# A mixture-of-experts pass on one core: one branch per unit for further blocks, their activations transposed a pass later, and six experts per loop turn in place of two

## The chip, the cores and the metric

One core of one Trainium2 chip runs the whole program. The metric is the device time of one execution in microseconds (us), the median of several runs.

## What is computed

A decoder layer for 512 tokens of width 1024: a token-mixing sub-layer (two attention branches), then a channel-mixing one, a mixture of 32 experts of which each token uses four. The change touches only the experts:

```python
logits = (ht @ w_router + b_router); top_val, top_idx = lax.top_k(logits, TOP_K)   # TOP_K = 4, 32 experts
# token slots are sorted by expert, each expert's group padded to blocks of 128 rows
def expert_block(args):
    xb, e = args
    gu = xb @ w_gate_up[e] + b_gate_up[e]            # 1024 -> 2 x 1024
    return clamped_swiglu(gu) @ w_down[e] + b_down[e]
ys = lax.map(expert_block, (xs, block_e)).reshape(n_rows, d) * row_w
out = zeros.at[row_tok].add(ys)
```

Each expert has about 64 tokens, so most have one block of 128 rows ("the first block"). Where a block beyond it is filled it is called a further block; up to three are provided for. In the profiled data three experts, numbers 7, 19 and 28, have one further block each: the trace shows 35 gathers for 32 experts.

## The kernel before

**Units and halves.** An expert has 12 MB of float32 weights in 12 *halves* of 1 MB (128 x 2048): eight for gate and up (`N_GU = 8`), four for down (`N_D = 4`). Two halves make one *unit*, 512 output columns accumulated in a PSUM bank. Each float32 factor is split in two parts of lower precision, so that a product is three matmuls (`multiply`, lines 1051 to 1053: `wh` x `xh`, `wl` x `xh`, `wh` x `xl`); a half is 12 matmuls of 128x512, a unit 24, with one bias matmul ahead (`biased`, line 1057).

**Engines.** SyncE loads the halves into eight slots `rawm` (`load`; a slot is free when `half_used` says that TensorE has used the half eight before). ScalarE rounds each to `wh` (four slots, line 1154, free when the half four before is used), VectorE forms `wl` = `rawm` - `wh` (line 1225). GpSimd gathers the tokens of an expert into `xy`, and scatters its outputs to `expert_rows` (lines 1315 and 1334); a gather waits for the scatter that frees the buffer.

**A pass.** `body(e, ...)` on TensorE is: the four gate/up units of expert e; the transposes of the tokens of e + 1 (`tokens_transposed`); the two down units of e - 1; the transposes of the activations of e (`act_transposed`). ScalarE and VectorE copy each transposed block into a high part (`xh`, `ah`) and a low part (`xl`, `al`). ScalarE's order in a body is written out: 12 weight splits, with the gate at halves 1 and 5, the tokens' high part at 7, the outputs of e - 1 at 9 and 11, and the activations' high part (`act_high`) last; VectorE's likewise.

**Further blocks.** Counts are data. Each engine loads the number of further blocks of an expert from `nk` into a register (`Expert`, line 874), and code for them stands inside branches: `further` (line 909) skips three copies of the work if there is none. In `blocks` the further ones come ahead of the first block, in `first_then_further` behind it. On TensorE, `gate_up_half_used` and `down_half_used` call it once for each of the 12 halves; with the two kinds of transposes a body has 14 such branches.

**The loop.** `passes` runs body 0, then the bodies of experts 1 to 30 two per turn in a hardware loop (line 943, 15 turns, with a hint for the backward branch), then body 31. Every engine but GpSimd runs through it, each on its own; GpSimd has a loop of its own, which doesn't change.

## Time and profile before

| | |
|---|---|
| median of 3 runs | 1965.25 us (1964.48 to 1971.41) |
| profiled execution | 1966.11 us, span of its instructions 1964.3 us |
| TensorE (PE) busy | 1700.9 us, 87% |
| VectorE (DVE), ScalarE (ACT), GpSimd (POOL) busy | 67%, 52%, 12% |
| granted TensorE clock, mean | 0.925 |
| DMA | 498.81 MB, 254 GB/s |

The profile comes from one execution. Matmuls overlap, so a matmul's duration (0.39 us) is longer than the distance between two (0.23 us). "Issue" is time in which an engine waited for nothing that the profile shows, neither a semaphore nor a buffer; its sequencer (marked q) may still be at work on branches and registers. The granted clock is given as a share: 1.00 is 2.4 GHz, 0.50 is 1.2 GHz. Until about 480 us attention runs, then the experts, and from 1903 us on the outputs are combined.

### The profile page before, as it was taken

What the parts mean: (1) busy time and instruction counts of PE and PEld (TensorE: products, weight loads), DVE (VectorE), ACT (ScalarE), POOL (GpSimd) and SP (SyncE); (2) the same over time, 40 slices, a digit from 0 to 9 for tenths busy, and PEclk for the clock granted to TensorE, in tenths of its full rate; (3) what the DMA queues carried; (4) which work ended last, traced back from release to release, by engine and by line L of the source; (5) the groups of instructions that cost most, each with busy time, mean ns of one, the idle gap of its engine ahead of it and who ended that gap; (6) DMA issues with size and microseconds to landing.
All of it is one profiled execution on the core that took longest, in us unless ns stands there. A gap on an engine that the chain in (4) does not pass through costs nothing.

```text
span 1964.3 us, 24736 instructions
## 1 busy us (share of the span) xinstructions
PE 1700.9 (87%) x7526; PEld 1315.3 (67%) x7527; DVE 1317.5 (67%) x1024; ACT 1029.6 (52%) x922; POOL 229.2 (12%) x232
## 2 busy tenths in 40 slices
PE   6999976685488999999999999999999998989860
PEld 1788854443376877787777877878787787778650
DVE  0444468644478778586877877866687787566645
ACT  2322234511366766465766766745576676455530
POOL 2000000102201001011111101101100111001110
PEclk9999987797699999999999999999999999999885
DMA  7675440012689999687989988977798899667735
GB/s 230 218 246 185 150 120 1 28 65 76 230 300 333 326 327 337 221 300 279 353 309 323 353 315 319 370 255 259 273 373 317 315 362 331 219 237 274 274 135 220
DMA packets 245582, 498.81 MB, mean 254 GB/s; under 512 B 16795, under 2 KB 17927, under 8 KB 244737
## 3 DMA queue, kind: packets, MB, share of 16 engines
q1 hardware_dynamic: 228288, 458.26, 65.5%
q0 software_dynamic: 14448, 34.73, 5.2%
q8 instruction: 217, 3.56, 0.7%
q10 hardware_dynamic: 2610, 2.11, 0.3%
q14 instruction: 19, 0.16, 0.0%
HBM read 490.23 MB, written 27.09 MB: 263 GB/s over the span
## 4 chain that ended last, share of the span: by engine, by line
PE 69%; issue 5%; DVE 3%; DMA 2%; ACT 1%; POOL 1%; POOLq 0%; ACTq 0%; DVEq 0%
PE ps L1051 20%; PE ps L1052 20%; PE ps L1053 19%; PE ps L621 3%; PE ps L993 3%; PE ps L1057 3%; DMA x1e<-x_after_mixing 1%; ACT wh L1154 1%; DVE wl L1225 1%; DMA xy<-h_ffn,icur 1%; DMA expert_rows<-xy,icur 1%; PE ps L641 0%; DVE yo L1388 0%; PE ps L634 0%; ACT h2t L692 0%
## 5 line engine op out<-in xcount | busy, mean ns | idle before, releaser
L1225 DVE TENSOR_TENSOR wl<-rawm,wh 128x2048 fp32r<-128x2048 f32 x384 | 876.2, 2290 | 318.9 <-ACT wh L1154 316.9
L1154 ACT ACTIVATE wh<-rawm 128x2048 fp32r<-128x2048 f32 x384 | 736.2, 1918 | 488.9 <-PE ps L1053 488.8
L1051 PE MATMUL ps<-wh,xh 128*128 128x512 f32 x1120 | 477.8, 427 | 0.0
L1052 PE MATMUL ps<-wl,xh 128*128 128x512 f32 x1120 | 447.4, 399 | 0.0
L1053 PE MATMUL ps<-wh,xl 128*128 128x512 f32 x1120 | 446.3, 399 | 0.0
L1053 PEld LDWEIGHTS ps<-wh,xl 128*128 128x128 f32 x1120 | 216.9, 194 | 48.2
L1052 PEld LDWEIGHTS ps<-wl,xh 128*128 128x128 f32 x1120 | 217.9, 195 | 45.6
L1051 PEld LDWEIGHTS ps<-wh,xh 128*128 128x128 f32 x1120 | 219.3, 196 | 41.6
L1051 PE MATMUL ps<-wh,ah 128*128 128x512 f32 x560 | 235.0, 420 | 0.0
L1052 PE MATMUL ps<-wl,ah 128*128 128x512 f32 x560 | 220.4, 394 | 0.0
L1053 PE MATMUL ps<-wh,al 128*128 128x512 f32 x560 | 220.1, 393 | 0.0
L1331 POOL COPY icur<-stab 128x1 int32 (+1 forms) x35 | 49.6, 1417 | 1026.4 <-ACT xy L1194 1026.3
L1057 PE MATMUL ps<-bparts,sel 96*128 96x512 bf16 x210 | 85.1, 405 | 70.3 <-issue 54.8
L1053 PEld LDWEIGHTS ps<-wh,al 128*128 128x128 f32 x560 | 106.4, 190 | 23.3
L1052 PEld LDWEIGHTS ps<-wl,ah 128*128 128x128 f32 x560 | 106.8, 191 | 21.9
L1051 PEld LDWEIGHTS ps<-wh,ah 128*128 128x128 f32 x560 | 107.5, 192 | 20.3
L1711 DVE TENSOR_TENSOR wlf<-raw,whf 128x2048 fp32r<-128x2048 f32 (+1 forms) x18 | 39.1, 2174 | 100.7 <-ACT whf L1487 100.7
L1057 PEld LDWEIGHTS ps<-bparts,sel 96*128 (+1 forms) x210 | 20.5, 98 | 115.3 <-issue 110.3
L1590 PE MATMUL ps<-whf,hh 128*128 128x512 f32 (+1 forms) x192 | 71.3, 372 | 0.0
L1592 PE MATMUL ps<-whf,hl 128*128 128x512 f32 (+1 forms) x192 | 71.1, 370 | 0.0
L1591 PE MATMUL ps<-wlf,hh 128*128 128x512 f32 (+1 forms) x192 | 71.0, 370 | 0.0
L993 PE MATMUL ps<-ident,xy 128*128 128x128 f32 x280 | 38.4, 282 | 33.2 <-DMA xy<-h_ffn,icur 26.8
(224 smaller groups left out, 1658.2 us busy)
## 6 DMA issues: line engine op xcount, KB each, us to landing
rawm<-in_w_gate_up SPq DMA_DIRECT2D x256, 1024.0 KB, 6.6
rawm<-in_w_down SPq DMA_DIRECT2D x128, 1024.0 KB, 6.3
raw<-in_w_ada SPq DMA_DIRECT2D x24, 1024.0 KB, 5.3
raw<-in_w_in SPq DMA_DIRECT2D x16, 1024.0 KB, 5.2
yt<-expert_rows POOLq DMA_DIRECT2D x4, 2048.0 KB, 9.1
wo<-in_w_out SPq DMA_DIRECT2D x2, 2048.0 KB, 17.0
bias_vectors_repeated<-bias_vectors POOLq DMA_DIRECT2D x1, 2304.0 KB, 15.8
xs<-in_x ACTq DMA_DIRECT2D x1, 2048.0 KB, 24.5
```

Of the source, the lines that this page charges most:

```text
L621: ins = nc.tensor.matmul(ps[:, 2 * b + half, :], src[:, k, t * P:(t + 1) * P], wo[:, 4 * b + k, half * UN:(half + 1) * UN], start=(k == 0) ...
L993: ins = nc.tensor.transpose(turned(b)[:, k // 4, (k % 4) * P:(k % 4 + 1) * P], src[:, k * P:(k + 1) * P], ident[:])
L1051: nc.tensor.matmul(dst, a_h[:, b, kk, :], wh[:, place.split(v), k, :], start=False, stop=False)
L1052: nc.tensor.matmul(dst, a_h[:, b, kk, :], wl[:, place.slot(v), k, :], start=False, stop=False)
L1053: ins = nc.tensor.matmul(dst, a_l[:, b, kk, :], wh[:, place.split(v), k, :], start=False, stop=kk == KC - 1)
L1057: nc.tensor.matmul(dst, sel[:, bass.ds(e, 1)].to_broadcast([96, P]), bias, start=True, stop=False)
L1154: nc.scalar.activation(flat(wh[:, place.split(v), :, :]), flat(rawm[:, place.slot(v), :, :]), ACT.Copy).then_inc(wh_done, 1)
L1225: nc.vector.tensor_tensor(flat(wl[:, place.slot(v), :, :]), flat(rawm[:, place.slot(v), :, :]), flat(wh[:, place.split(v), :, :]), ALU.sub ...
L1331: nc.gpsimd.tensor_copy(icur[:, 1, b:b + 1], stab[:, b, bass.ds(x.e + 1, 1)]).then_inc(scur[m], 1)
L1590: nc.tensor.matmul(dst, a_h, b_h, start=first, stop=False)
L1591: nc.tensor.matmul(dst, a_h, b_l, start=False, stop=False)
L1592: return nc.tensor.matmul(dst, a_l, b_h, start=False, stop=last)
```

## The change

Three edits. The loop of `passes` holds six bodies per turn (`TURN = 6`, five turns for experts 1 to 30). On TensorE `gate_up_used` and `down_used` work on a whole unit: one branch for the further blocks, which do both halves, then the first block's two halves. The activations of the first block are transposed ahead of the last 12 matmuls of the second down unit; those of further blocks in the next pass, behind its first gate/up unit (`further_act_transposed`), with their copies after half 1 on ScalarE and VectorE, and TensorE's wait for them ahead of the fourth unit (`further_acts_split`). The bank pair `turned(0)` serves all activations.

```diff
+TURN = 6
     def passes(eng, body):
 
         body(0, Place(0, 0), False)
-        with nc.Fori(0, E // 2 - 1, engines=[eng.engine], hint_back_edge=True) as k:
-            body(2 * k + 1, Place(3 * k + 1, 0), True)
-            body(2 * k + 2, Place(3 * k + 2, 4), True)
-        k = E // 2 - 1
-        body(E - 1, Place(3 * k + 1, 0), True)
+        with nc.Fori(0, (E - 2) // TURN, engines=[eng.engine], hint_back_edge=True) as k:
+            for i in range(TURN):
+                body(TURN * k + 1 + i, Place(3 * TURN // 2 * k + (3 * i + 2) // 2, 4 * (i % 2)), True)
+        body(E - 1, Place(3 * (E // 2 - 1) + 1, 0), True)
...
                     if b == 1 and not begins:
-                        acts = Expert(pe, e - 1).prefix() + START
...
-                        pe.wait_ge(al_done[1], acts)
...
-        def act_transposed(x, last):
+        def first_act_transposed(x, last):
 
             pe.wait_ge(xl_done[0], x.e + (1 if last else 2) + START)
+            pe.wait_ge(act_ready[0], x.count(T_GU, 1, 0))
+            transposed(turned(0), actv[:, 0, :], at_done[0])
+
+        def further_act_transposed(x):
             def work(b):
...
+                pe.wait_ge(act_ready[1], x.count(T_GU, 1, b))
+                pe.wait_ge(al_done[0], x.count(1, 0, 0))
+                pe.wait_ge(al_done[1], x.count(1, 0, b) - 1)
+                transposed(turned(0), actv[:, b, :], at_done[1])
+            x.further(work)
+
+        def further_acts_split(x):
+            with pe.If(x.more >= 1):
+                x.prefix()
+                pe.wait_ge(al_done[1], x.all_more(1, 0))
+                pe.sem_inc(passed, 1)
...
+        def gate_up_used(x, has_d, place, v):
...
+                biased(dst, x.e, bias)
+                for h in range(2):
+                    pe.wait_ge(wl_done, place.count(v + h))
+                    ins = multiply(dst, place, v + h, b, h, xh, xl)
+                ins.then_inc(gu_more, 1)
+            x.further(further)
+
+            if v == 0:
+                pe.wait_ge(xl_done[0], x.count(1, 0, 0))
+            if t == 0 and has_d:
+                pe.wait_ge(y_half_copied[up], x.e - 1 + START)
+            elif t:
+                pe.wait_ge((u_ready if up else g_ready)[0], x.count(T_GU, 0, 0))
+            biased(summed(0, up), x.e, bias)
+            for h in range(2):
+                pe.wait_ge(wl_done, place.count(v + h))
+                multiply(summed(0, up), place, v + h, 0, h, xh, xl).then_inc(half_used, 1)
...
+            for h in range(2):
+                if t and h and after is not None:
+                    first_act_transposed(after, is_last(after.e))
+                pe.wait_ge(wl_done, place.count(v + h))
+                multiply(summed(0, t), place, v + h, 0, h, ah, al).then_inc(half_used, 1)
...
         def body(e, place, has_d):
             x = Expert(pe, e)
             last = is_last(e)
...
+            before = None
+            for v in range(0, N_GU, 2):
+                if v == 2 and has_d:
+                    before = Expert(pe, e - 1)
+                    further_act_transposed(before)
+                if v == 6:
+                    if has_d:
+                        further_acts_split(before)
                     nxt = None if last else Expert(pe, e + 1)
...
+                gate_up_used(x, has_d, place, v)
             if not last:
                 tokens_transposed(nxt, e + 1)
...
-            act_transposed(x, last)
+            if has_d:
+                for t in range(U_D):
+                    down_used(before, x, place, N_GU + 2 * t, t)
+            else:
+                first_act_transposed(x, last)
...
                 split_high(place, v + SPL)
+                if v == 1 and has_d:
+                    act_high(before, before.further)
```

## Rows read from the trace of the kernel before

**Rows 1.** The page, part 4: the chain that ended last, by engine.
```profile
PE 69%; issue 5%; DVE 3%; DMA 2%; ACT 1%; POOL 1%; POOLq 0%; ACTq 0%; DVEq 0%
```

**Rows 2.** Windows by stage, experts 1 to 31: busy (x count) per engine, clock, DMA.
```profile
core 0: us, PE busy (x) PEld busy (x) DVE busy (x) ACT busy (x) POOL busy (x), PEclk, DMA share, GB/s
...
556.30:1903.00 1346.70, 1270.44 (x5685) 1020.85 (x5686) 1008.84 (x576) 842.17 (x577) 158.70 (x132) 0.97 0.84 301
```

**Rows 3.** Waits of TensorE, 560 to 1900: total us, times, longest.
```profile
PE ps L1057 <- issue: 54.6, 20, 7.2
...
PE ps L1057 <- DVE wl L1225: 5.2, 2, 4.4
```

**Rows 4.** The chain before expert 15: start us, us, what.
```profile
1136.46 4.47 issue
1140.93 0.60 PE ps L1057
```

**Rows 5.** Line 909, 1133 to 1142: duration ns min/median/max, first and last start.
```profile
L909 PEldq COMPARE_BRANCH  x3: 231/233/4590, 1133.2 to 1141.1; - x3
L909 ACTq COMPARE_BRANCH  x2: 92/95/98, 1135.6 to 1136.5; - x2
```

**Rows 6.** Line 943, the same stretch, TensorE's sequencer.
```profile
L943 PEldq COMPARE_BRANCH  x1: 1316/1316/1316, 1133.6 to 1133.6; - x1
```

**Rows 7.** DMA queues, 1062 to 1141: packets, MB, share of 16 engines.
```profile
q8 instruction: 13, 0.21, 1.0%
```

**Rows 8.** Windows of TensorE: body 14; first unit of expert 15; first unit of 14.
```profile
core 0: us, PE busy (x), PEclk, DMA share, GB/s
1099.51:1135.42 35.91, 35.91 (x167) 1.00 0.99 354
...
1140.93:1148.94 8.01, 8.01 (x25) 0.69 0.27 90
1100.38:1106.06 5.68, 5.68 (x27) 1.00 0.90 310
```

**Rows 9.** Windows, transposes' start to second unit: expert 14; 8; 19's first unit alone.
```profile
1099.51:1106.06 6.55, 6.55 (x34) 1.00 0.92 321
...
854.38:862.60 8.22, 7.58 (x42) 1.00 0.76 243
1299.50:1310.89 11.39, 11.39 (x50) 1.00 0.61 221
```

**Rows 10.** The same at ten backward branches: before 9, 29, and sum of ten.
```profile
903.37:911.27 7.90, 6.71 (x34) 1.00 0.51 165
...
1744.12:1759.87 15.75, 9.97 (x42) 0.78 0.52 178
sum 126.45, PE 86.78; mean PE 8.68
```

**Rows 11.** The same before 7, 13, 19, 25, 31: 13, and sum of five.
```profile
1057.13:1070.14 13.01, 9.25 (x34) 0.74 0.56 198
...
sum 66.61, PE 51.69; mean PE 10.34
```

**Rows 12.** Line 874, 775 to 779.5: TensorE's loads of a count.
```profile
L874 PEldq TENSOR_LOAD <-nk x2: 298/300/302, 775.9 to 777.4; - x2
```

**Rows 13.** Timeline of TensorE: transposes of expert 7's further tokens.
```profile
779.32 1.09 PE L993 MATMUL ps<-ident,xy 128*128 128x128 f32 x8 [3.23 <-issue]
```

**Rows 14.** Line 909 in body 14, 1100 to 1135.
```profile
L909 PEldq COMPARE_BRANCH  x13: 222/227/2173, 1100.0 to 1133.2; - x13
```

**Rows 15.** Timeline of GpSimd in body 14: the gather.
```profile
1111.78 2.63 POOL L1315 DMA_INDIRECT xy<-h_ffn,icur  x1 [0.90 <-POOL icur L1312]
```

**Rows 16.** DMA issues, 1110 to 1123: median us from issue to landing.
```profile
xy<-h_ffn,icur POOLq DMA_INDIRECT x1, 8.4
```

**Rows 17.** Timelines of TensorE: token transposes in bodies 30 and 9.
```profile
1829.67 1.97 PE L993 MATMUL ps<-ident,xy 128*128 128x128 f32 x8 [5.23 <-DMA xy<-h_ffn,icur]
...
928.79 1.09 PE L993 MATMUL ps<-ident,xy 128*128 128x128 f32 x8 [0.26 <-DMA xy<-h_ffn,icur]
```

**Rows 18.** Window of TensorE: experts 21 and 22.
```profile
1408.76:1484.51 75.75, 72.11 (x333) 1.00 0.99 362
```

**Rows 19.** Timeline of TensorE: the entry into the loop, expert 1.
```profile
556.31 0.61 PE L1057 MATMUL ps<-bparts,sel 96*128 96x512 bf16 x1 [0.26 <-issue]
```

More of the change, by code:

```diff
@@ L989, in experts_pe, with transposed @@
         pe.wait_ge(nk_ready, 1)
-        def transposed(b, src, done):
+        def transposed(banks, src, done):
             for k in range(KC):
-                ins = nc.tensor.transpose(turned(b)[:, k // 4, (k % 4) * P:(k % 4 + 1) * P], src[:, k * P:(k + 1) * P], ident[:])
-            ins.then_inc(done[min(b, 1)], 1)
+                ins = nc.tensor.transpose(banks[:, k // 4, (k % 4) * P:(k % 4 + 1) * P], src[:, k * P:(k + 1) * P], ident[:])
+            ins.then_inc(done, 1)
         def tokens_transposed(x, e):
@@ L1057, in biased, with further @@
             nc.tensor.matmul(dst, sel[:, bass.ds(e, 1)].to_broadcast([96, P]), bias, start=True, stop=False)
-        def gate_up_half_used(x, has_d, place, v):
-            t, up, h = v // 4, v // 2 % 2, v % 2
-            pe.wait_ge(wl_done, place.count(v))
-            def work(b):
+        def gate_up_used(x, has_d, place, v):
+            t, up = v // 4, v // 2 % 2
+            bias = bparts[:, up * D + UN * t:up * D + UN * (t + 1)]
+            def further(b):
                 dst = summed(b, up)
-                if v == 0 and b == 0:
-                    pe.wait_ge(xl_done[0], x.count(1, 0, 0))
-                if v == 0 and b:
+                if v == 0:
                     outputs = Expert(pe, x.e - 1).prefix() * U_D + START if has_d else None
@@ L1087, in work @@
-                ins = multiply(dst, place, v, b, h, xh, xl)
-                if b == 0:
-                    ins.then_inc(half_used, 1)
-                elif h:
-                    ins.then_inc(gu_more, 1)
-            x.blocks(work)
-        def down_half_used(x, after, place, v, d):
-            t, h = d // 2, d % 2
-            pe.wait_ge(wl_done, place.count(v))
-            def work(b):
+                if b == 1 and t:
+                    pe.wait_ge((u_ready if up else g_ready)[1], x.count(T_GU, 0, b))
+                elif b > 1 and up:
+                    pe.wait_ge(g_ready[1], x.count(T_GU, t, b))
+                elif b > 1 and t:
+                    pe.wait_ge(u_ready[1], x.count(T_GU, 0, b))
@@ L1100, in work, with down_used, further @@
+            biased(summed(0, up), x.e, bias)
+            for h in range(2):
+                pe.wait_ge(wl_done, place.count(v + h))
+                multiply(summed(0, up), place, v + h, 0, h, xh, xl).then_inc(half_used, 1)
+        def down_used(x, after, place, v, t):
+            bias = bparts[:, 2 * D + UN * t:2 * D + UN * (t + 1)]
+            def further(b):
                 dst = summed(b, t)
-                if d == 0 and b == 0:
-                    pe.wait_ge(al_done[0], x.count(1, 0, 0))
@@ L1103, in work @@
-                if d == 0 and b:
+                if t == 0:
                     gate_ups = x.before + x.more if after is None else x.before + x.more + after.more
@@ L1110, in work @@
                     pe.wait_ge(u_ready[1], gate_ups * T_GU + START)
[L1111 to L1122 removed]
+                elif b > 1:
+                    pe.wait_ge(y_copied[1], x.count(U_D, 0, b))
+                biased(dst, x.e, bias)
+                for h in range(2):
+                    pe.wait_ge(wl_done, place.count(v + h))
+                    ins = multiply(dst, place, v + h, b, h, ah, al)
+                ins.then_inc(d_more, 1)
+            x.further(further)
+            if t == 0:
+                pe.wait_ge(al_done[0], x.count(1, 0, 0))
+            pe.wait_ge((u_ready if t else g_ready)[0], (x.e + (1 if after is None else 2)) * T_GU + START)
+            biased(summed(0, t), x.e, bias)
+            for h in range(2):
+                if t and h and after is not None:
+                    first_act_transposed(after, is_last(after.e))
+                pe.wait_ge(wl_done, place.count(v + h))
+                multiply(summed(0, t), place, v + h, 0, h, ah, al).then_inc(half_used, 1)
         tokens_transposed(Expert(pe, 0), 0)
@@ L1173, in gate, with act_high @@
             x.blocks(work)
[L1175 removed]
+        def act_high(x, blocks):
             def work(b):
@@ L1196, in outputs, with at_once @@
             x.blocks(work)
+        def at_once(work):
+            work(0)
         tokens_high(Expert(act, 0))
@@ L1214, in body @@
                     outputs(before, v // 2 - 4, place, v, after)
-            act_high(x)
+            act_high(x, at_once)
         passes(act, body)
         end = Expert(act, E - 1)
+        act_high(end, end.further)
         outputs(end, 0, LAST, 1, None)
@@ L1267, in experts_dve, with at_once @@
         dve.wait_ge(nk_ready, 1)
+        def at_once(work):
+            work(0)
         tokens_low(Expert(dve, 0))
@@ L1280, in body @@
                 split_low(place, v + SPL)
+                if v == 1 and has_d:
+                    act_low(before, before.further)
             if not has_d:
                 tokens_low(Expert(dve, e + 1))
-            act_low(x)
+            act_low(x, at_once)
         passes(dve, body)
+        end = Expert(dve, E - 1)
+        act_low(end, end.further)
     def experts_pool(pool):
```

66 lines of the change are left out of this document (10 added, 56 removed).

## The prediction

> **What bounds the kernel now.** I start with the page's chain of work that ended last. TensorE holds 69% of it and "issue" 5%: time in which TensorE waited for nothing that the profile shows [rows 1]. The windows by stage put two thirds of the run, 1346.70 us, into the passes of experts 1 to 31, with TensorE busy for 1270.44 us of them at a mean clock of 0.97 [rows 2]. So TensorE bounds this stage, and the only thing to win is its 76 us of idle time and the slow clock behind it. TensorE's waits there are few: 54.6 us in 20 waits before the bias matmul (line 1057) are "issue"; the weights (`wl`) make it wait twice, 5.2 us [rows 3].
>
> Where are the "issue" waits? The chain around one of them, before expert 15, shows 4.47 us of issue from 1136.46 on and then the first bias matmul of the new expert [rows 4]. In the same 9 us the branch instructions tell why: TensorE's sequencer needs 1.3 us for the loop's backward branch (line 943), then 4.59 us for one skip branch of line 909, the first after it, where the median one takes 0.23 us [rows 5, 6]. The loop target was there in time; the code that the first skip leads to was not. The instruction queue moved 13 packets and 0.21 MB, so 16 KB each, in the two passes of that turn [rows 7]: TensorE's code doesn't stay on the chip, it streams. ScalarE takes 0.1 us for the same branches [rows 5].
>
> The price of one turn is more than the gap: the first unit behind it takes 8.01 us at clock 0.69, where an undisturbed one takes 5.68 at 1.00 (0.5 is 1.2 GHz, 1.00 is 2.4) [rows 8]. So I measure from the transposes' start to the second unit's start: 6.55 us undisturbed, 8.22 with 16 transposes, 11.39 plus 0.87 where the new expert has a further block [rows 9].
>
> Inside a turn nothing is lost: body 14 runs 35.91 us with TensorE busy for 35.91 [rows 8]. That is 144 matmuls, six biases and 16 transposes at full rate.
>
> **Part 1, six experts per turn.** Thirty experts (1 to 30) make 15 turns now: 14 backward branches and one exit. Afterwards there are 5 turns: 4 backward branches (before experts 7, 13, 19, 25) and the exit before 31. The ten that go (before 3, 5, 9, 11, 15, 17, 21, 23, 27, 29) last 126.45 us in sum [rows 10]; undisturbed they would last 9 x 6.55 + 8.22 = 67.2. Gain: **59.2 us**. The five that stay hold 66.61 us against 3 x 6.55 + 2 x 12.26 = 44.2, so 22.4 us of loss remain [rows 11]; those before 7 and 19 cost only 2 us each, because these experts have a further block and the first skip isn't taken.
>
> **Part 2, first activations transposed ahead of the last 12 matmuls of the down product.** The work (0.87 us) is the same. Its input waits were over long before (none shows within body 14 [rows 8]), and ScalarE reads the result after the last output as now, so nothing later comes earlier. They wait for the next expert's `xl` and for this one's activations, and the last 12 matmuls and the next unit queue behind them; both are done some 8 us before. What changes is the cover of a backward branch. The sequencer runs ahead of TensorE: the branch behind the last transposes starts at 1133.2, TensorE ends them at 1136.46 [rows 4, 5], a lead of some 3 us. Eight transposes last 0.87 us, 12 matmuls 2.7, so the queue holds more time later. I take 1.4 us off each of the three long edges left (13, 25, 31): **-4 us**, between 0 and -8. At the end, after expert 31, the wait for `al` stays: it hangs on ScalarE's last weight split and output, not on the transposes. Nothing.
>
> **Part 3, further activations in the next pass.** Three experts (7, 19, 28) have one further block. Today its 8 transposes follow the first block's directly: 8.22 - 6.55 = 1.67 us, of which 0.87 is the work. Behind the first unit the sequencer is ahead and the other 0.8 us are covered: **-2 us** in all, bounds 0 and -2.4. The added wait for `al` stands ahead of the fourth unit, with all of that unit queued behind it, 11 us after the transposes; two copies on ScalarE and VectorE fit in, so it costs nothing. Without that cover it would be 2 to 3 us in each of three passes. The token transposes of a further block lose one prefix sum, two register loads of 0.3 us each and their arithmetic, out of gaps of issue of up to 3.23 us [rows 12, 13]: another **-2 us** over three experts.
>
> **Part 4, one branch per unit.** A body has 12 + 2 taken skips now, 6 + 3 later. At 0.23 us each this would be 5 x 31 x 0.23 = 36 us, if it were exposed. It isn't: body 14 holds 13 such branches, one of them 2.17 us long, and TensorE isn't idle for any [rows 8, 14]. I book zero; the cover is the lead of the sequencer over the matmuls. The Trainium skill ("Advanced Engine Details and Errata", Control Flow Timing) gives 108 ns for a compare-and-branch; by it the same count would be 17 us, and equally hidden. The trace disagrees with the figure for taken skips, with 0.23.
>
> The other side is that skips become longer. I estimate from the source: a body holds some 1330 tensor instructions (12 halves x 4 copies x 24, plus transposes and biases) and perhaps 200 for control; two bodies over 13 to 14 fetches [rows 7] give some 225 per 16 KB. A skip then jumps about 95 instructions (0.4 of a fetched block) now and 170 (0.75) later, while a unit runs 56. Run and skip together remain one block per 5.7 us, against a full miss of 4.59. So fetches keep up on average, but a landing near a block's end exposes what the lead doesn't cover, at most 4.59 - 3 = 1.6 us. Six bodies have six alignments against two now. I book **+4 us**; bounds: 0 (body 14's loss; less isn't possible) and 1 us in every body, +31.
>
> The Trainium skill's rule here ("Runtime: NRT & Kernel Launch", Instruction fetch mechanics) is that a taken branch whose target lies outside the two resident pages must fetch it first. The trace agrees at the loop (4.59 us). Taken alone, it speaks for fewer turns and against longer skips; that is the slower rival below.
>
> **Part 5, what comes late next.** Tokens. Body 14's gather is issued at 1111.78 and takes 8.4 us, so it lands at 1120.2 [rows 15, 16], and its transposes are due after four units of 5.7 us from 1100.38 on, at 1123.2: 3 us of slack, 0.9 less once the other transposes move. Two bodies behind an expert with a further block the two scatters delay it: body 30 waits 5.23 us, and body 9, which had a backward branch to hide it, 0.26 [rows 17]. Body 9 loses that cover, 7.90 - 6.55 = 1.35 us [rows 10], and the 0.87 of the moved transposes: with the 0.26 that is 2.5 us. Body 21 in the same way +0.9, body 30 +0.9 more, small ones +1: **+5 us**, up to +15.
>
> ScalarE, VectorE and SyncE get three times the code per turn and may have to fetch at the five edges, which no row of theirs shows now (0.1 us [rows 5]). By TensorE's row a miss is 4.59 us. The order on all queues is unchanged, and the weights are prepared far enough ahead that TensorE waits for them twice in the stage [rows 3]. **+2 us**, bounds 0 and 5 x 4.6 = 23, nearer the lower, since TensorE mostly stands still at the same edges.
>
> Sum: -59.2 - 4 - 2 - 2 + 0 + 4 + 5 + 2 = **-56.2 us**. The profiled execution took 1966.1 us (span 1964.3), 0.9 above the median of 1965.25, so 1965.25 - 56.2 = **1909 us**.
>
> **Rivals.** *A, DMA takes over as the bound.* Each 6 us stall is also a rest for DMA: share 0.5 to 0.58 in those windows [rows 10, 11], 0.99 in body 14 [rows 8]. If a body needed 37 us of transfers against 35.9, the 25 or so undisturbed bodies would cost 1.1 us each: 27 us, result 1936. Against it: experts 21 and 22 ran 75.75 us with no long stall, DMA at 0.99 and 362 GB/s, TensorE busy for 72.11 [rows 18], and body 14 needs only 354 GB/s. Chance 0.11.
>
> *B, slower: longer skips expose the fetch inside bodies.* Place: the skip branch of each of 6 x 31 units. It cancels the gain from 0.3 us exposed per unit on. If every second unit exposed a full miss less the lead, 4.59 - 3.3 = 1.3 us, it would be 93 x 1.3 = 121 us on top of the forecast: 2030. For it: skips of 0.75 block nearly always cross into the next one. Against: 2.17 us waits are hidden now, and the fetch rate needed falls slightly. Chance 0.05; half of it (0.3 exposed) would be no change.
>
> *C, partial exposure:* 1 us per body, +27 over the forecast: 1936. Chance 0.10.
>
> *D, the change doesn't do what it says:* the stall belongs to the amount of code, not to the backward branch, and reappears inside the long turn: 1958 or so. Against: in all turns it sits on the first skip behind line 943, and the entry into expert 1 shows only 0.26 us [rows 19]. Chance 0.03.
>
> *E, better:* the loop target lies early in its block, so the first longer skip still lands in it: the edges 13, 25 cost nothing, 1899. Chance 0.08.
>
> Forecast 0.63. **Range:** 1890 to 1942 takes in E and the upper ends of A and C, leaves out B and D. A measurement here tells about 0.5% (10 us) from no change. Faster 0.92, same 0.03, slower 0.05.
>
> **What the new profile would show.** Right: "issue" before line 1057's successor falls from 20 waits to about 7, with 3 over 3 us; clock over the stage 0.99; the stage near 1290 us; DMA share there 0.88. Wrong: TensorE idle in front of biases inside turns with PE branches over 4 us (B, C); waits for `wl` or ScalarE waiting for rawm landings (A); tokens late by over 3 us in many bodies.

## The result, and the profile after

| | median us | range, runs |
|---|---|---|
| before, beside it | 1968.26 | 1964.48 to 1971.41, 4 |
| after | 1945.6 | 1941.11 to 1948.16, 4 |

Ratio 0.9883, 95% interval 0.9852 to 0.9914. The kernel became faster, by 22.7 us or 1.2%, where 56 were forecast, and 1945.6 lies outside the range of 1890 to 1942. The profiled execution took 1943.69 us, span 1941.2.

The page of the changed kernel, its parts 3 and 4: the queue that brings code to TensorE (packets, MB, share), and the chain by engine, to be held against [rows 1].

```profile
q8 instruction: 201, 3.29, 0.7%
...
PE 65%; DMA 5%; issue 5%; DVE 2%; POOL 2%; ACT 1%; POOLq 1%; ACTq 0%; DVEq 0%
```

The share of "issue" hasn't fallen, and DMA has risen from 2 to 5%. Next the window from expert 1's first bias matmul to the last matmul, and TensorE's waits in it.

```profile
core 0: us, PE busy (x) PEld busy (x) DVE busy (x) ACT busy (x) POOL busy (x), PEclk, DMA share, GB/s
560.65:1880.30 1319.65, 1259.09 (x5687) 1006.38 (x5686) 1006.37 (x576) 840.48 (x577) 178.65 (x132) 0.98 0.86 307
```

```profile
engine line waited for: us in total, times, longest us
PE ps L1054 <- issue: 22.9, 11, 3.8
PE ps L993 <- DMA xy<-h_ffn,icur: 18.5, 5, 5.6
PE ps L1048 <- issue: 8.7, 4, 2.8
...
PE ps L993 <- issue: 4.6, 3, 1.8
```

Against [rows 2, 3]: the stage is 27.1 us shorter, not 56. "Issue" ahead of the bias matmul (line 1054 now) fell from 54.6 us in 20 waits to 22.9 in 11. One line is new: 8.7 us of issue ahead of line 1048, a matmul that has no skip right before it or stands in the middle of a unit. Waiting for gathered tokens has risen to 18.5 us in 5 waits, from 5.5 us in 2.

**The edges did what was forecast.** The timeline of TensorE at three of the five edges that are left, before experts 7, 13 and 25, and windows of three first units (the last two behind the edges 31 and 25) and of one gap:

```profile
789.47 0.39 PE L1054 MATMUL ps<-bparts,sel 96*128 96x512 bf16 x1 [1.62 <-issue]
...
1054.53 0.39 PE L1054 MATMUL ps<-bparts,sel 96*128 96x512 bf16 x1 [1.00 <-issue]
...
1549.65 0.50 PE L1054 MATMUL ps<-bparts,sel 96*128 96x512 bf16 x1 [3.84 <-issue]
```

```profile
core 0: us, PE busy (x), PEclk, DMA share, GB/s
1082.18:1089.85 7.67, 7.67 (x27) 0.78 0.40 126
1823.99:1832.33 8.34, 8.34 (x25) 0.66 0.31 101
1549.65:1556.94 7.29, 7.29 (x26) 0.77 0.35 91
...
1078.38:1082.18 3.80, 0.00 (x1) 1.00 1.05 391
```

The five gaps are 1.62, 1.00, 0.91, 3.84 and 3.48 us, 10.9 in sum; the units behind 25 and 31 take 7.29 and 8.34 us against 5.68 undisturbed [rows 8], another 4.3. That makes 15.2 us for the five, where the forecast kept 22.4 - 4 = 18.4.

**Inside the turns something new stands.** The first and the last row of the windows above are no edge: they belong to this stretch of the chain, inside body 13. Below it, the branch instructions of line 910 (the skip) around it, and the window of the gap of [rows 4] in the kernel before.

```profile
1077.51 0.87 PE ps L993 x8
1078.38 3.80 issue
1082.18 0.61 PE ps L1054
```

```profile
engine op xcount: duration ns min/median/max, first and last start us, forms
L910 PEldq COMPARE_BRANCH  x2: 358/3385/6412, 1075.1 to 1075.5; - x2
```

```profile
1136.46:1140.93 4.47, 0.00 (x1) 0.79 1.01 356
```

The skip starts at 1075.5, lasts 6.41 us, and TensorE has been out of work since 1078.38. DMA moves 391 GB/s in the gap, and the unit behind it runs at a granted clock of 0.78 and takes 7.67 us. It is the picture of [rows 4, 5], but with no backward branch near it; DMA was as busy in that gap of the kernel before. Ten gaps of issue stand inside bodies, 1.12 to 3.80 us, 20.8 us in sum. Six stand ahead of line 1054, each behind a skip of 4.4 to 6.4 us. With the slow clock behind them, counted against 0.2265 us a matmul, the ten cost 28 us.

The other four (8.7 us) stand ahead of line 1048, and there the last skip was over in 0.22 to 0.39 us. The largest, 2.79 us ahead of the matmul at 852.22, has TensorE's sequencer at line 1089, in the middle of a unit's plain code:

```profile
L1089 PEldq FUSED_REGOPS  x1: 51/51/51, 846.3 to 846.3; - x1
L1089 PEldq ALU_OP  x1: 32/32/32, 852.3 to 852.3; - x1
```

Between the two rows, 5.9 us apart, TensorE runs dry at 849.43, though the sequencer waits for no semaphore there, and the last skip before them, at 845.6, took 0.37 us. So a stall can also stand in the code that a skip has led to, with no long branch to be seen. That it is a fetch too is inferred: these four gaps are absent where the same code is shifted or halved (below).

**Tokens come late.** GpSimd's timeline in body 9 and TensorE's first transposes there:

```profile
904.19 1.55 POOL L1353 COPY icur<-stab 128x1 int32 x1 [42.60 <-ACT xy L1203]
...
907.67 1.75 POOL L1353 COPY icur<-stab 128x1 int32 x1
910.31 2.13 POOL L1356 DMA_INDIRECT expert_rows<-xy,icur  x1 [0.89 <-POOL icur L1353]
918.91 1.25 POOL L1334 COPY icur<-gtab 128x1 int32 x1 [6.46 <-DMA expert_rows<-xy,icur]
921.05 2.67 POOL L1337 DMA_INDIRECT xy<-h_ffn,icur  x1 [0.90 <-POOL icur L1334]
```

```profile
929.35 1.97 PE L993 MATMUL ps<-ident,xy 128*128 128x128 f32 x8 [5.13 <-DMA xy<-h_ffn,icur]
```

Every step waits for the one before: a copy of indices, a scatter, a copy, a scatter, its landing, a copy, the gather. Bodies 9, 21 and 30 wait 5.1, 5.6 and 5.1 us; with two small ones and the slow clock behind them tokens cost 26.2 us, against 9.5 before.

| term, us of loss in the expert stage | before | after | forecast of the difference | measured |
|---|---|---|---|---|
| edges (14 and the exit, now 4 and the exit) | 81.6 | 15.2 | -59.2 - 4 | -66.4 |
| further activations' transposes | | | -2 | -2.4 |
| further tokens' transposes | 15.2 | 11.1 | -2 | -4.1 |
| code fetched inside bodies | 0 | 28 | +4 | +28 |
| tokens late | 9.5 | 26.2 | +5 | +16.7 |
| other engines' code at the edges | | | +2 | 0 |
| sum | | | -56.2 | -28.2 |

The stage from the first token transposes to the last matmul went from 1388.6 to 1360.5 us, -28.1, so the table closes. The other 5.2 us of difference lie ahead of the experts: their first transposes start at 519.6 us instead of 514.4, in code that the change doesn't touch. This is taken up with the shifted kernel below.

### The profile page after: what moved, and what is told of

Its sections match the earlier page's. It is cut to its first block, busy times and chain, and to the rows that moved or that the text cites. A ratio compares the mean times of both kernels' runs of the same rounds, so it can differ in the third digit from the quotient of the medians.

```text
span 1941.2 us, 24261 instructions
## 1 busy us (share of the span) xinstructions
PE 1693.3 (87%) x7526; PEld 1305.4 (67%) x7527; DVE 1315.4 (68%) x1024; ACT 1027.8 (53%) x922; POOL 249.1 (13%) x232
## 3 DMA queue, kind: packets, MB, share of 16 engines
q1 hardware_dynamic: 228288, 458.26, 66.4%
q8 instruction: 201, 3.29, 0.7%
## 4 chain that ended last, share of the span: by engine, by line
PE 65%; DMA 5%; issue 5%; DVE 2%; POOL 2%; ACT 1%; POOLq 1%; ACTq 0%; DVEq 0%
PE ps L1048 18%; PE ps L1050 18%; PE ps L1049 18%; PE ps L993 3%; PE ps L622 3%; PE ps L1054 2%; DMA xy<-h_ffn,icur 2%; DMA expert_rows<-xy,icur 1%; DMA x1e<-x_after_mixing 1%; POOL icur L1353 1%; PE ps L642 0%; POOL icur L1334 0%; DVE yo L1410 0%; ACT wh L1163 0%; PE ps L424 0%
## 5 line engine op out<-in xcount | busy, mean ns | idle before, releaser
L1163 ACT ACTIVATE wh<-rawm 128x2048 fp32r<-128x2048 f32 x384 | 736.3, 1918 | 450.9 <-PE ps L1050 446.0
L1048 PE MATMUL ps<-wh,xh 128*128 128x512 f32 x1120 | 468.1, 418 | 7.6 <-issue 5.3
L1050 PE MATMUL ps<-wh,xl 128*128 128x512 f32 x1120 | 440.4, 393 | 0.2 <-issue 0.2
L1049 PE MATMUL ps<-wl,xh 128*128 128x512 f32 x1120 | 440.0, 393 | 0.0
L1048 PEld LDWEIGHTS ps<-wh,xh 128*128 128x128 f32 x1120 | 214.4, 191 | 49.1 <-issue 6.2
L1050 PEld LDWEIGHTS ps<-wh,xl 128*128 128x128 f32 x1120 | 212.5, 190 | 47.8 <-issue 1.3
L1049 PEld LDWEIGHTS ps<-wl,xh 128*128 128x128 f32 x1120 | 213.3, 190 | 43.2
L1048 PE MATMUL ps<-wh,ah 128*128 128x512 f32 x560 | 239.3, 427 | 3.4 <-issue 3.4
L1054 PE MATMUL ps<-bparts,sel 96*128 96x512 bf16 x210 | 84.0, 400 | 30.9 <-issue 22.9
L1337 POOL DMA_INDIRECT xy<-h_ffn,icur x35 | 68.1, 1947 | 31.7 <-POOL icur L1334 28.2
## 6 DMA issues: line engine op xcount, KB each, us to landing
wo<-in_w_out SPq DMA_DIRECT2D x2, 2048.0 KB, 16.9
```

Of the source, the lines that this page charges most:

```text
L1048: nc.tensor.matmul(dst, a_h[:, b, kk, :], wh[:, place.split(v), k, :], start=False, stop=False)
L1049: nc.tensor.matmul(dst, a_h[:, b, kk, :], wl[:, place.slot(v), k, :], start=False, stop=False)
L1050: ins = nc.tensor.matmul(dst, a_l[:, b, kk, :], wh[:, place.split(v), k, :], start=False, stop=kk == KC - 1)
L1054: nc.tensor.matmul(dst, sel[:, bass.ds(e, 1)].to_broadcast([96, P]), bias, start=True, stop=False)
L1163: nc.scalar.activation(flat(wh[:, place.split(v), :, :]), flat(rawm[:, place.slot(v), :, :]), ACT.Copy).then_inc(wh_done, 1)
L1337: pool.indirect_dma_start(out=xy[b][:], out_offset=None, in_=h2_d, in_offset=bass.IndirectOffsetOnAxis(ap=icur[:, 0, b:b + 1], axis=0), bo ...
```

## The experiments

Beside the kernels before and after, eleven others ran, and the kernel before was profiled once more. Each ratio is against runs of the kernel before on the same chip, whose medians were 1968.3 beside the changed kernel and 1969.8, 1966.9, 1965.2 and 1968.1 in the four sets of experiments. Times of different sets are best compared by their ratios. In this section "issue" and "tokens" are the sums of TensorE's idle time from 560 us to the last matmul in the view of waits, and "stage" runs from the first token transposes to the last matmul.

| kernel | us | ratio, interval | stage | issue | tokens |
|---|---|---|---|---|---|
| before | 1965 to 1970 | | 1388.6 | 61.0 | 5.5 |
| before, shifted | 1982.11 | 1.0069, 1.0047 to 1.0091 | 1400.6 | 71.6 | 6.9 |
| before, six per turn alone | 1938.84 | 0.9846, 0.9812 to 0.9879 | 1360.4 | 40.2 | 15.2 |
| after | 1945.6 | 0.9883, 0.9852 to 0.9914 | 1360.5 | 36.4 | 18.5 |
| after, shifted | 1928.41 | 0.9823, 0.9801 to 0.9845 | 1349.4 | 24.5 | 17.5 |
| after, two per turn | 2049.3 | 1.0402, 1.0364 to 1.044 | 1476.2 | 126.8 | 5.6 |
| the same, shifted | 1937.47 | 0.9869, 0.9823 to 0.9915 | 1356.0 | 34.8 | 13.9 |
| after, indices early | 1919.22 | 0.9741, 0.9703 to 0.9779 | 1349.8 | 43.7 | 3.0 |
| after, code for one further block | 1898.93 | 0.9656, 0.9613 to 0.9698 | 1318.5 | 10.0 | 13.8 |
| the same, own output buffers | 1871.62 | 0.9521, 0.9493 to 0.955 | 1291.3 | 4.8 | 0 |
| indices early, branches per half | 1885.72 | 0.9599, 0.957 to 0.9627 | 1306.1 | 14.6 | 0.4 |
| the same, shifted | 1919.73 | 0.9763, 0.9733 to 0.9792 | 1345.9 | 32.6 | 0.4 |
| the same unshifted, ten per turn | 1882.43 | 0.9582, 0.9562 to 0.9603 | 1304.7 | 12.1 | 1.1 |

**The long turn alone.** The kernel before with the new loop and nothing else:

```
-        with nc.Fori(0, E // 2 - 1, engines=[eng.engine], hint_back_edge=True) as k:
...
+        with nc.Fori(0, (E - 2) // TURN, engines=[eng.engine], hint_back_edge=True) as k:
+            for i in range(TURN):
+                body(TURN * k + 1 + i, ...
```

> The kernel before with the six-expert loop alone; branches stay one per half, and activations are transposed where they were. Theory F (the stalls inside the turns of the changed kernel come from the longer skip per unit, which lands near the end of a fetched block of code): skips are as short as before, so in-body stalls that end with issue or sit behind a long TensorE branch stay under 5 us in sum against some 28 in the changed kernel; ten backward branches go (-59); tokens get late once the DMAs rest less (about +12): about 1918 to 1925 us, faster than the changed kernel by some 20. Rival R (the stalls come because the code fetches no longer find idle DMA queues in a long turn): in-body stalls of 20 us and more here too, about 1940 to 1945 us.

Measured 1938.84 us, 14 us above the expected 1918 to 1925. Inside bodies no gap of issue ahead of a bias matmul is over 0.7 us, and they sum to 3.9 us, so at this place of the code long turns don't bring the stalls of the changed kernel by themselves, and neither does a DMA that rests less. But its four backward branches before 7, 13, 19 and 25 leave gaps of 7.83, 8.15, 5.30 and 7.27 us, and the tokens of bodies 9, 21 and 30 are late by 4.8 to 5.5. The backward branch (line 944) over all passes, in this kernel and in the changed one:

```profile
L944 PEldq COMPARE_BRANCH  x5: 89/5690/6261, 780.9 to 1823.8; - x5
```

```profile
L944 PEldq COMPARE_BRANCH  x5: 89/556/1292, 784.4 to 1817.1; - x5
```

Same loop, same hint, 5.7 us or 0.56 us in the median: the code ahead of the branch differs, and with it the place of the branch. The late tokens come with this part of the change.

**The short skips' replacement alone.** The changed kernel with two experts per turn:

```
-TURN = 6
+TURN = 2
```

> The changed kernel with two experts per turn: branches once per unit and further activations a pass later, but 15 turns. Theory F: stalls inside the two bodies too, 1 us per body on average, beside 15 edges; these are shorter than before by the cover of 12 matmuls (some 4 instead of 5 us each): 1965 to 1985 us. Rival R: no stall inside the bodies, edges shortened only: 1945 to 1955 us.

Measured 2049.3 us: 79 us slower than the kernel before, where 1965 to 1985 was expected. TensorE's waits to the last matmul:

```profile
PE ps L1054 <- issue: 117.6, 40, 5.4
PE ps L993 <- DMA xy<-h_ffn,icur: 5.6, 2, 5.1
```

Three gaps per turn, of 1.3, 1.7 and 4.7 us in the turn of 605 to 643: the first two behind skips of 4.4 us, the third behind a backward branch of 3.95 us and a skip of 2.90. The 14 edges hold 59 us of the gaps, so some 60 us stand inside bodies. It looks like rival B, priced at 2030 with a chance of 0.05, but that price was for six experts per turn, without the ten edges, so the two numbers are close by luck. Either the longer skips do it, or the place where they land.

**Where the code lies.** The same kernel with 128 instructions more on TensorE ahead of the experts. By the prediction's estimate of some 225 instructions to the 16 KB of a packet [rows 7] that is about half a packet.

```
     def experts_pe(pe):
         pe.wait_ge(nk_ready, 1)
+        for _ in range(128):
+            pe.sem_inc(passed, 1)
```

> The kernel with two experts per turn and branches per unit (2049 us, 38 stalls behind long branches, 116 us), with 128 idle increments of an unused semaphore on TensorE ahead of the experts: all its code moves by half a fetched block. Theory F (place of a skip's landing in its block decides): the pattern of stalls per turn, now 1.5, 1.9 and 4.3 us, changes in every turn alike; the time moves by tens of us, most likely down, 1950 to 2030 us. Rival (length of the skip alone, or the branches' own time, decides): the same stalls at the same places, 2045 to 2055 us.

Measured 1937.47 us: 112 us less, or 105 by the two ratios, from instructions that compute nothing, and below the 1950 to 2030 that was expected.

```profile
PE ps L1056 <- issue: 31.3, 15, 4.0
PE ps L995 <- DMA xy<-h_ffn,icur: 13.9, 5, 5.1
```

The skips are as long as before and the loop is as short. So the place decides, and with only two bodies per turn the same bad places come back in most of the fifteen turns.

**The same shift on the changed kernel, on the one with branches per half, and on the kernel before.** The first:

> The changed kernel with 128 semaphore increments on TensorE ahead of the experts, 64 bytes each, so that the code of the passes lies 8 KB further against the 16 KB that one packet of the instruction queue brings. Theory A (a taken skip stalls where it lands in a block that isn't there yet, so where the code lies decides): the stalls behind long branches of line 912 or so inside bodies (28 us in the changed kernel) fall on other bodies and units, and the time moves by more than 8 us, either way; from the shift of the form with two experts per turn (38 stalls became 13) I expect the sum between 5 and 60 us. Theory B (the stalls come from DMA load at those moments, not from where the code lies): the same bodies show them, time within 6 us of 1945. The 128 increments themselves last about 128 x 0.06 = 8 us at most and lie beside other engines' work or add up to 8 us.

Measured 1928.41 us, 17 less, or 12 by the two ratios to the kernel before. The stalls do move. Waits to 1820 us:

```profile
PE ps L995 <- DMA xy<-h_ffn,icur: 17.5, 6, 5.5
PE ps L1056 <- issue: 16.4, 5, 4.2
PE ps L995 <- issue: 5.2, 3, 1.7
PE ps L1052 <- issue: 2.9, 2, 2.5
```

Of the ten gaps inside bodies two are left, 0.5 and 2.5 us, both after 1805. In exchange three of four backward edges now cost what the fourth did: 4.09, 4.18, 4.03 and 3.89 us of gap, where the changed kernel has 1.62, 1.00, 0.91 and 3.84. DMA load doesn't choose the places: the work and its order are the same.

This run also bears on the 5.2 us ahead of the experts. Its first token transposes start at 511.3 us, though the added instructions stand before them in the program's order and spread over 19.4 us (490.0 to 509.4) beside other engines' work, where 8 at most was expected. The window 262 to 395 of the changed kernel, and of the shifted one (us, TensorE busy, clock, DMA):

```profile
262.00:395.00 133.00, 85.64 (x444) 0.71 0.18 54
```

```profile
262.00:395.00 133.00, 85.69 (x455) 0.78 0.18 54
```

The granted clock there differs, 0.71 to 0.78, in a stretch whose instructions are all the same; over all profiles the experts begin between 511 and 520 us. So the 5 us aren't counted as an effect of the three edits. Why the clock is granted differently stays open. The second profile of the kernel before was taken to see whether executions of one kernel spread so far:

> The kernel before, profiled once more. In its first profile the experts' first transposes start at 514.4 us, in the changed kernel's at 519.6, though the code up to there is the same. If that is the spread between executions, they start at about 519 here, the losses at the loop's edges are those of the first profile within 5 us, and the span is some 1969 us; if it belongs to the kernel, 514.4 again.

It took 1962.9 us, experts from 514.8 on, stage 1384.7. That is 514.4 again and not 519, so by the test of its expectation the difference belongs to the kernel and not to the execution. No other kernel was profiled twice, and the kernel before, shifted, starts at 519.3 with the same code up to there; what decides stays open.

The kernel before, shifted:

> The kernel before, shifted by the same 128 increments of 64 bytes. If the place of the code against the 16 KB packets sets the stalls of every form, this one moves too: either the 14 edges (76 us now) become cheaper or dearer, or stalls appear inside bodies, where there are none now; the time moves by more than 10 us either way. The shifts so far moved the time by -112, -17 and +34 us. If only forms with branches per unit or long turns are open to it, the time stays within 8 us of 1965.

Measured 1982.11 us, ratio 1.0069: slower than unshifted, 14 us against the runs beside it, as the first of its two expectations has it. Its waits to 1820 us, and its backward branch over all passes:

```profile
PE ps L1059 <- issue: 48.5, 19, 5.5
PE ps L1053 <- issue: 14.4, 13, 1.7
```

```profile
L943 PEldq COMPARE_BRANCH  x15: 89/4167/5684, 631.0 to 1862.2; - x15
```

Thirteen gaps appear inside bodies, ahead of line 1053, where [rows 8] had none, and the miss at the edge moves from the first skip onto the backward branch: 4.2 us in the median here against 0.77 unshifted (1.3 in the one of [rows 6]). What I had read as a property of turns of two, "inside a turn nothing is lost", was the place of that code. Place isn't all of it, though. Turns 1 and 3 of the changed kernel run the same code, neither with a further block, and yet the first has gaps of 1.27, 1.88 and 1.12 us inside its bodies and the third of 3.80 and 1.69, of which the 3.80 stands at a skip that costs nothing in turn 1. What decides beside the place no run separates.

**Half the code.** The branches for second and third further blocks are left out; no expert here has more than one further block, and an input that needs more would not be computed.

```
-                for b in range(2, NB):
+                for b in range(2, 2):
                     with self.eng.If(self.more >= b):
```

> The changed kernel with code for one further block in place of three; a third and fourth block of an expert, which no expert of this data fills, is left out. A skip jumps a third of the instructions and a body is about half as long in code. Theory F: in-body stalls behind long TensorE branches vanish (28 us) and the edges cost 5 us less: 1905 to 1915 us, with some 110 code fetches of TensorE in place of 200. Rival R: fewer fetches help in the same direction but only in part, 1925 to 1935 us. Rival S (stalls are not code at all but counts loaded into registers): no change, 1940 to 1945 us.

Measured 1898.93 us, below the expected 1905 to 1915. The code queue, and the waits to the last matmul:

```profile
q8 instruction: 111, 1.82, 0.4%
```

```profile
PE ps L993 <- DMA xy<-h_ffn,icur: 13.8, 5, 5.4
...
PE ps L1054 <- issue: 4.9, 3, 3.5
```

Fetched packets fall from 201 to 111 and all gaps for code inside bodies are gone; one of 3.5 us is left at the exit. The stage is 42.0 us shorter than in the changed kernel: 26.4 of it are issue, 4.7 tokens, 7.6 the slow clock by my count, and 3 are not accounted for. Fewer fetches and no gaps in bodies go together, as they must if code is what TensorE waited for. It was run at one place of the code only, so how much of the gain is the amount and how much the place isn't separated.

**Indices early.** The changed kernel, with GpSimd's copies of the indices moved ahead of the waits for the outputs and for the scatter's landing:

```
                 pool.sem_inc(passed, 1)
                 nc.gpsimd.tensor_copy(icur[:, 0, b:b + 1], gtab[:, b, bass.ds(x.e + 1, 1)]).then_inc(gcur[m], 1)
                 pool.wait_ge(gcur[m], x.count(1, 0, b))
+                if done is not None:
+                    pool.wait_ge(y_out[m], stored if b else done.stored(0))
```

> The changed kernel; GpSimd copies the row indices of a gather and of a scatter before it waits for the scatter's landing or for the outputs, not behind. Theory T (the tokens are late because the chain output, scatter, gather is longer than four units once nothing else holds TensorE up): the chain loses 4.5 us (two copies of 1.2 to 1.8 us and two times 0.9 us behind them), so the waits of 5.1 to 5.6 us in bodies 9, 21 and 30 shrink to about 1 with no slow clock behind, some 18 us less than the changed kernel: 1925 to 1930 us. Rival (the transfers themselves are late, from full DMA queues): under 5 us gained.

Measured 1919.22 us, 26 less than the changed kernel (28 by the ratios), where 18 were expected. GpSimd in body 9:

```profile
902.46 1.82 POOL L1353 DMA_INDIRECT expert_rows<-xy,icur  x1 [44.34 <-ACT xy L1203]
904.29 0.20 POOL L1345 COPY icur<-stab 128x1 int32 x1
905.40 2.54 POOL L1353 DMA_INDIRECT expert_rows<-xy,icur  x1 [0.91 <-POOL icur L1345]
907.94 1.38 POOL L1330 COPY icur<-gtab 128x1 int32 x1
914.52 2.01 POOL L1335 DMA_INDIRECT xy<-h_ffn,icur  x1 [5.20 <-DMA expert_rows<-xy,icur]
```

From the first scatter to the gather's issue it takes 12.1 us, where the changed kernel needs 16.9 from its first copy on, and TensorE waits for tokens 3.0 us instead of 18.5. Its "issue" sum rose by 7 us meanwhile, mostly because gaps at the same skips are longer: 4.06 us where the changed kernel has 1.88, and 5.66 us, behind a skip of 8.35, where it has 1.69. Why they are longer wasn't separated. The profile is that of the slowest of four executions, 1932.32 us, whose stage is only 10.7 us shorter than the changed kernel's; where the other executions win the rest of the 26 us no trace shows.

**Own output buffers.** The kernel with half the code, whose outputs go to buffers of their own, so that the gather needn't wait for the scatters and is issued first:

```
-                nc.scalar.activation(xy[b][:, t * UN:(t + 1) * UN], summed(b, t),
+                nc.scalar.activation(xy[b + 2][:, t * UN:(t + 1) * UN], summed(b, t),
```

> The kernel with code for one further block, and outputs in buffers of their own: a gather waits for no scatter and is issued ahead of it in each pass. A third and fourth block of an expert, which this data doesn't fill, is left out. Theory T (tokens late because their buffer is freed by the scatter): all five waits for tokens go, 14.6 us, and the slow clock behind three of them, some 5 us: 1878 to 1884 us, DMA then at its highest share. Rival A (the DMAs become the bound once nothing rests): under half of that, and waits for wl or for rawm in its place.

Measured 1871.62 us, the fastest of all and below the expected 1878 to 1884. No wait for tokens is left, and none for weights has come in its place. Like the one above it holds for at most one further block.

**Short skips again, the rest kept.** Branches per half as in the kernel before, with the long turn, the moved transposes and the early indices:

```
+            x.further(further)
+
+            if v == 0:
+                pe.wait_ge(xl_done[0], x.count(1, 0, 0))
...
+            pe.wait_ge(wl_done, place.count(v))
+            multiply(summed(0, up), place, v, 0, h, xh, xl).then_inc(half_used, 1)
```

> The changed kernel with early indices (1919 us), but with branches per half again, as before; six experts per turn, the moved transposes and the deferred further activations stay. It tells the granularity of the branches apart from everything else. Theory F: the in-body stalls (some 23 us with their slow clock) nearly vanish, edges remain at 2 to 8 us each as their alignment falls: 1895 to 1908 us. Rival B (one branch per unit is worth its 0.23 us each): 1919 us or more.

Measured 1885.72 us, 33.5 less than with branches per unit and early indices (28 by the ratios), and below the expected 1895 to 1908. Taken by itself this says that short skips win. Shifted, it doesn't:

> The form with branches per half and early index copies (1885.7 us), shifted by the same 128 increments. Theory A: its skips are 95 instructions long instead of 170, so most land in a block that is already there, wherever the code lies: stalls inside bodies stay below 10 us in sum and the time within 10 us of 1886 plus the increments' own time. If it moves by 20 us or more, short skips were only lucky in the first alignment, and length explains nothing.

Measured 1919.73 us, 34 more (32 by the ratios), and the expectation's own test ("if it moves by 20 us or more, short skips were only lucky") has come out against short skips. Its waits to the last matmul, and one of its skips, ahead of a gap of 2.47 us:

```profile
PE ps L1050 <- issue: 12.9, 11, 2.5
PE ps L1056 <- issue: 11.5, 4, 4.4
```

```profile
L910 PEldq COMPARE_BRANCH  x2: 222/3174/6125, 677.1 to 683.5; - x2
```

The shorter skips (95 instructions by the prediction's estimate) miss as well, and for as long: 6.12 us here. The gaps are more but smaller (eleven ahead of line 1050 with 12.9 us) than the ten with 20.8 us in the changed kernel. Two alignments per form are too few to say which length is better on average: 1886 and 1920 with early indices stand against 1919 with early indices for branches per unit, of which no shifted run was made.

The unshifted one with ten experts per turn:

```
-TURN = 6
+TURN = 10
```

> Branches per half, early index copies, ten experts per turn in place of six: three turns, so the backward branches before 7, 13, 19, 25 give way to two before 11 and 21. In the form with six, these edges and the exit cost about 11 us in sum, the exit 3.8 of it. Expected gain 3 us, so 1883, within 1878 to 1890; by the theory of the forecast (an edge with a first block only costs 4.5 to 6 us with its slow clock) 1890, since both edges left have a first block only.

Measured 1882.43 us (1879.9 to 1884.99), against 1885.72 in another set of runs (1884.3 to 1887.01): the expected 3 us, and about the limit of what can be told. It is the fastest kernel here that still takes up to three further blocks, 4.2% under the kernel before.

## Why the prediction was wrong, point by point

- **What bounds the kernel, Parts 1 and 2: right.** Ten edges gone and three shortened were to bring 63.2 us and brought 66.4. The edge before 13 shrank to a gap of 1.0 us as argued; 25 and 31 kept 3.84 and 3.48. But the runs show that part of this was the place of the code: the edges of the long turn alone have gaps of 5.3 to 8.2 us, and after a shift three of the changed kernel's four cost 4 us each.
- **Part 3: right,** and a little small: -2.4 for the activations, -4.1 for the tokens.
- **Part 4: this is the step that failed.** I booked +4 us for fetches exposed inside bodies, with a bound of +31; 28 us were measured, practically the bound: ten gaps with 20.8 us, and some 7 us of slow clock behind them. Three points of it don't hold. "Fetches keep up on average": an average rate says nothing of a single landing, and a bad landing comes back in other turns: three gaps in turn after turn are what made 2049 us of the form with two. "At most 4.59 - 3 = 1.6 us" held roughly for five of the six gaps behind a skip (1.27 to 2.00 us, skips of 4.38 to 4.71), but the sixth was 3.80 us behind a skip of 6.41. The DMA share doesn't tell it apart: it was 1.01 in the gap of the 4.59 us skip and 1.05 in this one, and 0.98 to 1.05 in gaps behind skips of 4.4 to 4.7 us. What made it longer stays open. And the sum looked only at skips: four of the ten gaps, 8.7 us, stand in plain code behind a short skip, with up to 5.9 us between two rows of the sequencer.
- **The lower bound, and the value near it,** came from body 14, which loses nothing [rows 8]. That was evidence for one alignment. The shifted kernel before has thirteen gaps in such bodies.
- **Part 5, tokens: the mechanism was right, the size wrong.** +5 was booked, up to +15; +16.7 were measured. Body 9 was worked out as 0.26 + 1.35 + 0.87 = 2.5 us and waited 5.13. Of the missing 2.6, 2.2 are two index copies: 1.75 and 1.25 us in the timeline above, 0.20 and 0.64 in the trace of before, whose way from the first copy to the gather's issue was 14.66 us against 16.86. I had taken that chain as constant. The largest miss is body 21: 0.9 booked, 5.59 us waited. There the same way went from 13.52 to 16.86 us, and the cover of the backward branch before 21, 8.09 - 6.55 = 1.54 us, was left out of the working though body 9's was in. Body 30, booked at 6.1, waited 5.08.
- **Part 5, other engines: 2 us too many.** No branch of ScalarE, VectorE or SyncE lasts 0.5 us, the longest 0.17. A second instruction queue, q14, did go from 19 packets to 87, and has 86 with the long turn alone. ScalarE has five waits of issue, 4.6 us in sum, and VectorE one of 2.1 us that the kernel before hasn't, and TensorE waits for none of them.
- **The signs.** Forecast for the right case were a stage near 1290 us, clock 0.99, DMA share 0.88 and some 7 waits of issue with 3 over 3 us; it came to 1319.7, 0.98, 0.86, and 11 such waits with 4 more ahead of line 1048, 3 in all over 3 us. The sign named for B and C, idle TensorE ahead of biases inside turns with branches over 4 us, is there six times.
- **The rivals.** A (DMA as the new bound) fell: half the code ran the stage in 1318.5 us, own buffers in 1291.3, with the same transfers. The share of 0.5 to 0.58 that it gave to the stalls belongs mostly to the slow unit behind them (0.27 [rows 8]); in the gap itself DMA ran at 1.01. C, 1 us of exposure in each body for 1936 us, has the right sum, 28 us over 31 bodies, though in ten gaps and not in each body. The terms of the table give 1965.25 - 28.2 = 1937 us, which lies inside the range; the 5.2 us ahead of the experts, which no term covers, carry the measured time past its end. So that the time fell outside by 3.6 us is partly luck, while half of the forecast gain was missing in any case. D (the stalls reappear inside the long turn) is what happened in kind, at 28 us and not in full. E is out: the edge before 13 kept 1.0 us and that before 25 3.84. B did not happen here, but did in the kernel with two per turn: 2049 us. Its chance of 0.05 against C's 0.10 had no ground in the profile; both depended on the alignment, which no row of before could show. The range should have reached to C with the upper bound of the tokens, 1936 + 10.

The Trainium skill ("Runtime: NRT & Kernel Launch", Instruction fetch mechanics) states that code comes in blocks of 16 KB, read ahead in order, and that a taken branch out of the two blocks at hand must wait for its target. The traces agree in the main: 201 packets bring 3.29 MB, so 16 KB each, most stalls stand on taken skips and backward branches, and a shift of the code moves them. The sentence on branches doesn't name the four gaps in plain code behind a short skip, 8.7 us in the changed kernel. Read strictly it is a rule about targets and blocks, not about turns, and in that form it would have asked for the alignment of every skip. What it doesn't state is a price; here it is up to 8.35 us for a skip (indices early), and up to 8.2 us of idle TensorE where backward branch and skip miss one after the other.

## What to carry to other kernels

- Where code streams, each taken branch is a possible stall, and which ones stall depends on where the code lies against the fetched block. A comparison of two forms of such a kernel needs each at more than one shift: here 128 instructions that compute nothing moved four kernels by -105, -12, +14 and +32 us by the ratios, where the change itself moved the time by 23.
- Less code in the passes means fewer blocks to miss: half of it, at the one place tried, left a single gap of 3.5 us.
- Where stalls are removed, list the chains that ran in their shadow step by step, with the longest durations that their instructions show anywhere in the trace. Here GpSimd's small index copies, moved ahead of the waits, were worth 26 us in the median, and 11 in the profiled execution.

## What the runs showed of the hardware that was not expected

- TensorE's code shifted by 128 instructions, about half a packet of the instruction queue by estimate: from 2049.3 to 1937.47 us.
- TensorE ran out of work for 2.79 us in plain code, behind a skip that took 0.37 us: not every stall for code shows as a long branch.
- The backward branch, with the same hint, has a median of 0.35, 0.56, 0.77, 3.7, 4.2 or 5.7 us by kernel and placement.
- GpSimd's copy of 128 indices takes 0.20 us at one place and 1.2 to 1.9 at others: right behind a scatter's issue 1.75 in body 9 of the changed kernel, and 0.20 (body 9) or 1.90 (body 30) in the kernel before. What decides between them stays open.
